# Modulation as 48 dot products on VectorE instead of a tree of sums on GpSimd, and the first group's tokens repeated before the last query unit

## The reference, cut to what matters

```python
sh, sc, gt = jnp.split((s_lat @ w_mod[i] + b_mod[i])[:, None, :], 3, axis=-1)   # s_lat = silu(c), 1024 numbers
h = _rms(x, norm_g[i]) * (1.0 + sc) + sh                                        # w_mod[i]: 1024 x 3072, i = 0, 1
x = x + gt * mixer(h)
...
u = expert_u[it]                                   # expert layer: 8 heads x 16 of 16384 experts for each token
v = expert_v[it]
act = jax.nn.gelu(jnp.einsum("td,ted->te", xt, u), approximate=False)
return jnp.einsum("te,ted->td", gt * act, v)
```

## Time and profile before

| | us |
|---|---|
| median of 3 runs (lowest, highest) | 1314.91 (1311.63, 1318.79) |
| the profiled execution, its own time | 1313.33 |
| its span, first to last instruction | 1311.5 |
| PE busy in the span | 904.6 |
| DVE busy | 830.7 |
| POOL busy | 558.0 |
| ACT busy | 257.5 |

### The profile page before, as it was taken

How to read it: one execution, slowest core, us unless ns; L and a number is a source line. 1 busy time by engine, 2 the same in 40 slices (tenths; PEclk the granted TensorE clock), 3 DMA queues, 4 the chain that set the end, 5 groups by cost and what they waited for, 6 DMA issues and landing times. The chain is left out here.

```text
span 1311.5 us, 17486 instructions
## 1 busy us (share of the span) xinstructions
PE 904.6 (69%) x6828; PEld 688.4 (52%) x6828; DVE 830.7 (63%) x1942; ACT 257.5 (20%) x515; POOL 558.0 (43%) x440
## 2 busy tenths in 40 slices
PE   6449979997968889687634454434444499659998
PEld 6449958796756657456411131111211288538887
DVE  1975152237978968595478777777765489972311
ACT  3021101103352213221002111011100143412210
POOL 1858777974433433253244445444444034600000
PEclk9769979997879959788756565555655689869999
DMA  9636547758999999999999999999999414212341
GB/s 382 252 129 252 198 176 288 273 210 341 426 420 384 420 418 414 423 423 421 421 421 421 422 420 421 421 421 418 417 420 421 194 67 175 80 64 71 122 148 45
DMA packets 51266, 401.99 MB, mean 307 GB/s; under 512 B 5616, under 2 KB 7920, under 8 KB 8944
## 3 DMA queue, kind: packets, MB, share of 16 engines
q0 software_dynamic: 40320, 293.62, 54.5%
q1 hardware_dynamic: 10000, 104.57, 20.6%
q10 hardware_dynamic: 864, 2.68, 0.5%
HBM read 399.80 MB, written 1.05 MB: 306 GB/s over the span
## 5 line engine op out<-in xcount | busy, mean ns | idle before, releaser
L409 POOL DMA_INDIRECT arena<-uv_dram,arena x192 | 220.8, 1150 | 322.2 <-PE ps L552 276.4
L552 PE MATMUL ps<-arena 128*32 128x256 f32 x1536 | 157.4, 549 | 213.0 <-DVE arena L1410 213.0
L1394 DVE CUSTOM_DVE_ANT_0 arena<-arena 128x1024 f32<-128x1024 f32 x192 | 232.5, 1225 | 98.0 <-DMA arena<-uv_dram,arena 92.2
L552 PEld LDWEIGHTS ps<-arena 128*32 128x32 f32 x1536 | 51.5, 141 | 301.1 <-DVE arena L1410 255.8
L822 PE MATMUL ps<-xn,wring 128*128 128x256 f32 x640 | 147.6, 395 | 17.5 <-DVE arena L1738 9.9
L822 PEld LDWEIGHTS ps<-xn,wring 128*128 128x128 f32 x640 | 127.1, 199 | 38.0 <-issue 18.2
L458 PE MATMUL ps<-xn,wring 128*128 128x128 f32 x1024 | 129.2, 288 | 10.3 <-DMA wring<-units_dram 6.0
L458 PEld LDWEIGHTS ps<-xn,wring 128*128 128x128 f32 x1024 | 125.1, 203 | 18.6 <-issue 8.6
L409 POOL DMA_INDIRECT wring<-uv_dram,arena x64 | 79.2, 1238 | 108.6 <-PE ps L552 98.6
L941 ACT ACTIVATE gel<-dots 128x2 f32<-128x2 f32 x128 | 26.0, 203 | 471.1 <-DVE dots L1394 446.3
L552 PE MATMUL ps<-wring,arena 128*32 128x256 f32 x512 | 50.4, 530 | 72.6 <-DVE arena L1410 72.6
(11 more groups left out here) (244 smaller groups left out, 1319.0 us busy)
## 6 DMA issues: line engine op xcount, KB each, us to landing
wring<-units_dram SPq DMA_DIRECT2D x48, 2048.0 KB, 9.6
arena<-mod_dram POOLq DMA_DIRECT2D x24, 1024.0 KB, 6.2
arena<-uv_dram,arena POOLq DMA_INDIRECT x192, 14.2
hA<-x_t_dram SPq DMA_DIRECT2D x2, 512.0 KB, 5.4
arena<-mem_t_dram ACTq DMA_DIRECT2D x1, 1024.0 KB, 11.5
arena<-keys_dram ACTq DMA_DIRECT2D x2, 512.0 KB, 4.7
wring<-uv_dram,arena POOLq DMA_INDIRECT x64, 14.3
wring<-grp_dram SPq DMA_DIRECT2D x1, 1024.0 KB, 4.8
```

The lines of the kernel that those rows point to most:

```text
L409: pool.indirect_dma_start(ring[b], None, uv_d, bass.IndirectOffsetOnAxis(ap=idx[:, n:n + 1], axis=0)).then_inc(sem(f"row_in{b}"), 16)
L552: mm = pe.matmul(acc_ps(q)[G * c:G * (c + 1), :], lhsT=diag[:, s % 2, j, :], rhs=ring[b][:, D + 256 * c:D + 256 * (c + 1)], start=(p == 0 ...
L1394: post(V.tensor_tensor_reduce(out=ring[b][:, 0:D], in0=ring[b][:, 0:D], in1=x_rep[q % 2], scale=1.0, scalar=0.0, op0=ALU.mult, op1=ALU.add ...
```

## The change

Modulation moves off GpSimd and PE. Each chunk of `mod_w` now holds, for each of 128 partitions, two whole columns of 1024 weights; silu(c) is repeated on all partitions (512 KB, a new input `c`, in the place of `x_rep[1]`). One `tensor_tensor_reduce` on DVE multiplies 128 x 1024 weights by it and leaves the running sum in one column of `modc`: 48 of them, in DVE's `fill`, one at each of steps 12 to 25, two at each of steps 27 to 34, one at each of 35 to 40 and two at each of 41 to 46. GpSimd only issues the 24 chunks, into four buffers instead of two, each once the dots of the chunk four before are done; the first four wait for unit k instead of q. `modulation` moves from slot 4 to slot 0. For group 0 the repeated tokens are made from `first_x`, 32 tokens that DVE normalises by themselves after `pq0`, and PE and ACT do them before unit `pq1` instead of after the chain. At the start SP issues x of the first tile, the columns, q, the memory tokens, k, v and x of the second tile; ACT issues `small_w`, the constants and c.

```diff
@@ -86,10 +86,10 @@
-MOD_SUMS = 4
-MOD_STEP = {}
-for _i in range(MOD_CHUNKS):
-    MOD_STEP.setdefault(8 + (15 * _i) // 8, []).append(_i)
+MOD_BUFFERS = 4
...
+MOD_STEP = {**{s: 1 for s in range(12, 26)}, **{s: 2 for s in range(27, 35)}, **{s: 1 for s in range(35, 41)},
+            **{s: 2 for s in range(41, 47)}}
@@ -203,7 +202,7 @@
-        mod_w = area(4096, 4096).rearrange("p (s k n) -> p s k n", s=2, k=KB)
+        mod_w = area(4096, 8192).rearrange("p (s b d) -> p s b d", s=MOD_BUFFERS, b=2)
@@ -213,6 +212,7 @@
+        first_x = blocks(area(R + 1024, 256), KB)
@@ -236,7 +236,7 @@
-        mod_p = x_rep[1].rearrange("p (s n) -> p s n", s=MOD_SUMS)
+        silu_c = x_rep[1]
@@ -353,10 +353,8 @@
-            for t in range(TT):
-                sp.dma_start(hA[:, :, tokens(t)], x_t[:, :, tokens(t)]).then_inc(sem(f"x_in{t}"), 16)
-                if t == 0:
-                    sp.dma_start(cols[:], cols_d).then_inc(sem("cols_in"), 16)
+            sp.dma_start(hA[:, :, tokens(0)], x_t[:, :, tokens(0)]).then_inc(sem("x_in0"), 16)
+            sp.dma_start(cols[:], cols_d).then_inc(sem("cols_in"), 16)
@@ -376,6 +374,10 @@
+                if n == 0:
+                    sp.dma_start(mem_n, mem_t).then_inc(sem("mem_in"), 16)
+                if n == 2:
+                    sp.dma_start(hA[:, :, tokens(1)], x_t[:, :, tokens(1)]).then_inc(sem("x_in1"), 16)
@@ -384,21 +386,11 @@
-            pool.wait_ge(sem("w_in0"), 16)
-            for i in range(2):
-                pool.dma_start(mod_w[:, i].rearrange("p k n -> p (k n)"), mod_d[i]).then_inc(sem(f"mod_in{i}"), 16)
-            need(pool, "silu_c")
+            pool.wait_ge(sem("w_in1"), 16)
...
-                w = mod_w[:, i % 2]
-                pool.wait_ge(sem(f"mod_in{i % 2}"), 16 * (i // 2 + 1))
-                did(pool, pool.tensor_tensor(w, w, silu_c[:].unsqueeze(2).broadcast_to([P, KB, 256]), ALU.mult), "pool_step")
-                did(pool, pool.tensor_tensor(w[:, 0:4], w[:, 0:4], w[:, 4:8], ALU.add), "pool_step")
-                did(pool, pool.tensor_tensor(w[:, 0:2], w[:, 0:2], w[:, 2:4], ALU.add), "pool_step")
-                if i >= MOD_SUMS:
-                    need(pool, "mod_sum", i - MOD_SUMS + 1)
-                did(pool, pool.tensor_tensor(mod_p[:, i % MOD_SUMS], w[:, 0], w[:, 1], ALU.add), "mod_part")
-                if i + 2 < MOD_CHUNKS:
-                    pool.dma_start(w.rearrange("p k n -> p (k n)"), mod_d[i + 2]).then_inc(sem(f"mod_in{i % 2}"), 16)
+                if i >= MOD_BUFFERS:
+                    pool.wait_ge(sem("mod_dot"), 2 * (i - MOD_BUFFERS + 1))
+                pool.dma_start(mod_w[:, i % MOD_BUFFERS].rearrange("p b d -> p (b d)"), mod_d[i]).then_inc(sem(f"mod_in{i % MOD_BUFFERS}"), 16)
@@ -488,14 +480,6 @@
-            def mod_chunk(i):
...
-                need(pe, "mod_part", i + 1)
-                for j in range(2):
-                    mm = pe.matmul(ps[:, 7, 2 * i + j:2 * i + j + 1], lhsT=mod_p[:, i % MOD_SUMS, j * P:(j + 1) * P], rhs=cst("one"),
-                                   start=True, stop=True)
-                post(mm, "mod_sum")
@@ -517,7 +501,8 @@
-                        mm = pe.matmul(aux_ps[G * c:G * (c + 1), j * P:(j + 1) * P], lhsT=xn[:, 4 * i + j, G * q:G * (q + 1)],
+                        mm = pe.matmul(aux_ps[G * c:G * (c + 1), j * P:(j + 1) * P],
+                                       lhsT=xn[:, 4 * i + j, G * q:G * (q + 1)] if q else first_x[:, 4 * i + j, :],
@@ -765,6 +750,10 @@
+                if t == 0:
+                    need(pe, "first_x", 1)
+                    for i in range(2):
+                        repeated_tokens(0, i)
@@ -775,19 +764,10 @@
-                for i in MOD_STEP.get(at[0], ()):
-                    mod_chunk(i)
-            for s, chunks in MOD_STEP.items():
-                if s >= CHAIN_STEPS:
-                    for i in chunks:
-                        mod_chunk(i)
-            need(pe, "xn", 7)
-            for i in range(2):
-                repeated_tokens(0, i)
@@ -978,18 +958,18 @@
-                    act.dma_start(mem_n, mem_t).then_inc(sem("mem_in"), 16)
...
+                    act.dma_start(silu_c, c_d).then_inc(sem("c_in"), 16)
...
-                    act.wait_ge(sem("cols_in"), 16)
+                    act.wait_ge(sem("c_in"), 16)
...
-                    go(act.activation(silu_c[:], col("c", 0, KB), ACT.Silu), "silu_c")
+                    go(act.activation(silu_c, silu_c, ACT.Silu), "silu_c")
@@ -1374,8 +1354,8 @@
-                dve.wait_ge(sem("mod_sum"), MOD_CHUNKS)
-                go(V.tensor_tensor(modc[:], ps[:, 7, 0:48], col("b_mod", 0, 48), ALU.add), "mod_read")
+                dve.wait_ge(sem("mod_dot"), 2 * MOD_CHUNKS)
+                go(V.tensor_tensor(modc[:], modc[:], col("b_mod", 0, 48), ALU.add), "mod_read")
@@ -1395,7 +1375,7 @@
-                if s == 4:
+                if s == 0:
@@ -1661,6 +1641,8 @@
+                if t == 0:
+                    go(V.tensor_tensor(first_x, x[:, :, 0:G], r[:, :, 0:G].broadcast_to([P, KB, G]), ALU.mult), "first_x")
@@ -1679,6 +1661,14 @@
+                for m in range(counts.get("mod_dot", 0), counts.get("mod_dot", 0) + MOD_STEP.get(at[0], 0)):
+                    i = m // 2
+                    if m == 0:
+                        need(dve, "silu_c", 1)
+                    dve.wait_ge(sem(f"mod_in{i % MOD_BUFFERS}"), 16 * (i // MOD_BUFFERS + 1))
+                    w = mod_w[:, i % MOD_BUFFERS, m % 2]
+                    post(V.tensor_tensor_reduce(out=w, in0=w, in1=silu_c, scale=1.0, scalar=0.0,
+                                                op0=ALU.mult, op1=ALU.add, accum_out=modc[:, m:m + 1]), "mod_dot")
@@ -1873,13 +1863,13 @@
-    mod = np.ascontiguousarray(a["w_mod_2"].reshape(2, KB, P, 12, 256).transpose(0, 3, 2, 1, 4).reshape(MOD_CHUNKS, P, KB * 256))
+    mod = np.ascontiguousarray(a["w_mod_2"].reshape(2, D, 12, 2, P).transpose(0, 2, 4, 3, 1).reshape(MOD_CHUNKS, P, 2 * D))
-             "b_mod": a["b_mod_2"], "c": a["c_2"]}
+             "b_mod": a["b_mod_2"]}
```

More of the change, by code:

```diff
@@ L142, with build @@
 CONV_DVE = (0, 2, 3, 4, 6, 7)
-def build(nc, x_t, mem_t, cols_d, const_d, small_d, keys_d, units_d, grp_d, mod_d, uv_d, out_d, dbg=None):
+def build(nc, x_t, mem_t, cols_d, c_d, const_d, small_d, keys_d, units_d, grp_d, mod_d, uv_d, out_d, dbg=None):
     with ExitStack() as ctx:
@@ L168, in build @@
         warm = sb("warm", [P, 1])
-        silu_c = sb("silu_c", [P, KB])
         gl = sb("gl", [P, 4, NH])
@@ L559, in slot @@
                 if p in (10, 12) and q + 1 < GROUPS:
-                    if p == 10 and q + 1 == GROUPS // 2:
-                        need(pe, "xn", 14)
+                    if p == 10 and (q == 0 or q + 1 == GROUPS // 2):
+                        need(pe, "xn", 14 if q else 7)
                     repeated_tokens(q + 1, p // 2 - 5)
```

4 lines of the change are left out of this document (2 added, 2 removed).

## The result

The changed kernel takes 1272.44 us (median of 4 runs, 1270.91 to 1273.60) where the kernel before, on the same chip, takes 1316.85 (1311.63 to 1324.21): a ratio of 0.9655, 95% interval 0.9616 to 0.9694. The profiled execution took 1272.79 us, with a span of 1270.9; its span is 40.6 us shorter than that of before.

The account below looks back on a forecast made before the run. DMA bounds the gather stage; before it PE's chain does, slowed through DVE by GpSimd arithmetic. 23.8 + 6.8 + 5.1 + 1.5 + 3.2 + 7.2 - 0.5 - 2 = 45.1; 1313.3 - 45.1 = 1268 us, range 1255 to 1284.

Parts of the forecast that it names:

- Start, -23.8: Stretch up to the delta rule's first matmul: without GpSimd arithmetic, and with c landing at 25.4, it comes at 68, not 91.8.
- rival 2: Load order at the start: ACT's packets pass in one turn of many, c lands about 19.7, 1263 us; chance 0.06.
- rival 1: Load order at the start: ACT's queue gets half the bytes, c lands at 14.7, 1255 us; chance 0.1.
- The stand of 6.8: PE's wait at 178 us for DVE behind the short convolution L1591: claimed to go, -6.8 us.
- The same restart at 92 us is cheaper, -1.5: PE's slow running after its stand before the delta rule: cheaper since PE stands some 3 us, not 5.7; -1.5 us.
- After it PE ran slowly, -5.1: PE's slow matmuls from 185.6 us, behind its 6.8 us stand: claimed to return to full speed, -5.1 us.
- The waits for L1421 and the softmax, -3.2: PE-bound part: waits for L1421 shrink by 1.7 of 2.8 us, attention's softmax wait of 1.5 goes; -3.2 us.
- PE's sums, -7.2 for 20 chunks: PE-bound part: the modulation's matmuls (L495), 20 chunks outside the stand, no longer hold PE; -7.2 us.
- 48 dots, 0.5: DVE's 48 dots, 58.8 us in all, run while DVE would stand; 0.5 us of cost put in.
- Chunks late, 2: Steps 27 to 35: chunks come just in time, the one at step 35 some 4 us late; 2 us of cost.
- Rivals 3 and 4: Before the gathers: late chunk reloads hold DVE and PE, 1282 to 1303 (chance 0.18); dots don't hide, 1327 (chance 0.05).
- The gather stage moves the same bytes ... so it passes through whole.: From the first gather to the end: length unchanged at about 1010 us, so the whole 45.1 us gain reaches the total.

Follow-up runs that it names:

- the two other edits: Against the changed kernel: silu(c) moved ahead of the first silu of q, and the repeated tokens put back after the first tile's chain; 1258.23 us, ratio 0.9533.

## Why the prediction was right, and where its terms were off

**The forecast**, 1268 with 1255 to 1284, held: 1272.44. That the number came within 4.4 us is partly luck, since terms that were off had opposite signs (below). The mechanism, that GpSimd's arithmetic costs time through VectorE, is shown from both sides, by taking it out of before and by giving it back to the change. The Trainium skill has this, page "SBUF — State Buffer", section "Who interferes with whom": a VectorE instruction with two inputs in SBUF contends with a GpSimd instruction that reads SBUF, and one with at most one does not, outside the two-port modes that copies among others can enter. This case agrees on both halves. L1421, all in SBUF, took 2284 ns in before and 694 after the earlier trace rows; of the same size, but with one input in PSUM, in before up to 302 us:

```profile
L1551 DVE TENSOR_TENSOR arena<-arena,ps 128x512 f32<-128x512 f32 x9 | 6.2, 687 | 28.3 <-PE ps L507 27.7
...
L1431 DVE TENSOR_TENSOR hA<-ps,hA 128x512 f32<-128x512 f32 x4 | 2.8, 692 | 33.0 <-PE ps L458 33.0
```

That is the pace of the changed kernel (L1531 687 ns, L1411 692), though GpSimd computes in most of this stretch. A copy with one input, in SBUF (L1462, 12 columns), was slowed all the same, 3.35 us at 49.91 in before and 0.17 in the changed kernel; the exception allows that, but no row shows in which mode it ran.

**Start, -23.8.** The first delta matmul came at 67.17, not 68: -24.6. c landed at 25.8 (25.4 predicted), the memory sums began at 30.27 (29.7), the memory sums took 5.14 us behind the stand where they take 3.62 without one: 1.5 and not 2.5. The counting of rows that gave 25.4 is supported by small_w's 5.1 us, though it held only in the whole: small_w's turn in front of c cost 5.4 us and I had put it at about 3. The rule of the Trainium skill that the prediction set beside it (page "DMA: Bandwidth & Descriptors", section "Queues, rings and completion order") would have had c at 19.7; the trace says 25.8, so here it does not fit: rival 2 is out, and rival 1 (14.7) too.

**From there to the first gather, -21.3** (6.8, 5.1, 1.5, 3.2 and 7.2 less 0.5 and 2). It was 209.6 us (301.35 - 91.8) and is 185.6 (252.78 - 67.17): -23.9. The kernel of before without GpSimd's arithmetic splits it, 196.3 us (252.07 - 55.75): -13.2 by the arithmetic, for which I had 16.6, and -10.7 by PE's sums and all else, for which I had 4.7.
- The stand of 6.8 is gone, as forecast.
- "The same restart at 92 us is cheaper, -1.5": 0.9. The first quarter ends 6.6 us behind the first delta matmul, and 7.5 before.
- "After it PE ran slowly, -5.1": off. The slow rows from 185.63 to 197.69 (12.1 us) are now 149.30 to 158.23 (8.9 us), so 3.1 came back. PE had not stood, and still the granted clock fell to 0.69 from 153 to 158 us:

```profile
151.74 0.43 PE L670 MATMUL ps<-arena 64*128 64x64 f32 x2
152.01 1.43 PE L675 MATMUL ps<-arena 64*128 64x128 f32 x8
153.38 5.02 PE L474 MATMUL ps<-wring,arena 128*128 128x512 f32 x8
```

- The waits for L1421 and the softmax, -3.2: 2.8, by the waits shown. With the 6.8, 0.9 and 3.1 this makes 13.6, near the 13.2 measured.
- PE's sums, -7.2 for 20 chunks: 23 of the 24 pairs stand behind the first delta matmul once the long stand ahead of it is gone, and at 0.36 us they are 8.3.
- "48 dots, 0.5": at most 0.9 at the first gather, nothing in the median. "Chunks late, 2": nothing that shows. DVE waits 6.4 us for chunks in 4 times, and no wait of PE follows one of these. The longest is 3.2 us; the prediction had said none over 3. Rivals 3 and 4 are out. Of the 10.7, some 2.4 us (10.7 - 8.3) stay unassigned.

**"The gather stage moves the same bytes ... so it passes through whole."** This is the step that failed, and it is why 1268 was 4.4 us low: the bytes are the same, the time is 8 us longer (1018.1 against 1010.2). Both had been named as signs: 1010 us if right, another length if wrong. The prediction costed the repeated tokens by where PE stands ("the first slot starts as late as before") and not by what queues behind them: pq1, its buffer, unit k, and with it the second tile's chain. That the repeat's place divides the short stages from the long ones is shown; the link by unit k is argued. The first dot came 11.3 us behind the first gather, 9.35 before. Its own sum up to the gather was 3.5 us too small (48.6 against 45.1), and the two errors have opposite signs.

**Modulation in slot 0**, costed at nothing with 1 us without cover: with slot 4 the median is 3.1 us lower, and by itself that is inside the intervals (0.9577 to 0.9645 against 0.9616 to 0.9694). On top of the two other edits the median is 1.8 us lower, but the stage from the first gather only 0.5 (732.8 against 733.3). So a cost of up to 3 us is possible and not shown.

## What to carry to other kernels

An engine on which no long wait ends can be the costliest: compare the same instruction's mean in a stage with it and in one without, and look at the single pieces on the timeline too, since the mean hides how dense the overlap is. Freeing a helper engine of a wait can make the kernel slower, as it did here by 1.5%. When work is moved ahead of something, follow the buffer that this something frees, and don't cost a stage that is bound by transfers by its bytes alone; ask how early each request reaches it.

## What the runs showed of the hardware

- A two-input VectorE instruction of 128 columns took 346, 747, 1202 and 2129 ns on average, with GpSimd idle, computing with waits, with fewer waits, and without a pause. Twelve of them on end took 3.23 us while GpSimd stood, 17.8 to 18.4 beside the arithmetic of before, and 24.7 where that came without a pause.
- A VectorE instruction of 4 columns took 4.08 us beside GpSimd's product of 3.62 us, and 0.16 to 0.2 without GpSimd's arithmetic.
- A 32 KB transfer of 128 rows took 5.1 us at its turn in ScalarE's queue, beside SP's queue with rows of 16 KB; 512 KB in 128 rows took 5.6 us there.
- PE's granted clock was 0.69 for 153 to 158 us after sixteen matmuls of 64 columns and eight of 128 on end, with no stand ahead of them; it was 1.00 from 145 to 149. Which of these made it fall is not shown.
